# Reordering the input projection of a two-layer attention and RWKV-7 backbone

## The reference

```python
IN_SIZES = (ATTN_WIDTH, ATTN_WIDTH, ATTN_WIDTH,          # attention's q, k, v: 512 each
            RWKV_WIDTH, RWKV_WIDTH, RWKV_WIDTH,          # r, k, v of the RWKV heads: 512 each
            2 * DECAY_LORA, 2 * AAA_LORA, GATE_LORA)     # wd 64, ad 64, gd 96
r = _shift_mix(r, mu[0, 0], mu[0, 1])                    # k and v alike: a token mixes with both neighbours
v = v + (v_first - v) * jax.nn.sigmoid(v0 + (v @ v1) @ v2)      # second layer alone
kk = _heads(k * k_k)
kk = kk * lax.rsqrt(jnp.maximum(jnp.sum(kk * kk, axis=-1, keepdims=True), 1e-24))
for d in range(2):                                       # two directions
    wl = w0[d] + jnp.tanh(wd[..., d * 32:(d + 1) * 32]) @ w2[d]
    decay = jnp.exp(-jnp.exp(-jax.nn.softplus(-wl) - 0.5))
    a = jax.nn.sigmoid(a0[d] + ad[..., d * 32:(d + 1) * 32] @ a2[d])
    kd = kf * (1.0 + (a - 1.0) * k_a)
```

## Time and profile before

| | before |
|---|---|
| median of 3 runs | 2672.52 us (2670.89 to 2677.59) |
| the profiled execution | 2676.98 us, its span 2675.2 us |
| busy: PE, DVE, ACT, POOL | 91%, 62%, 45%, 6% |
| mean granted TensorE clock | 0.957 |
| DMA | 497.56 MB, 186 GB/s; 281 to 372 GB/s in the slices of the experts |
| MATMUL L635 (projection's channels) | x736, 301.6 us, 569 ns each |

### The profile page before, as it was taken

How to read it: one execution, slowest core, us unless ns; L and a number is a source line. 1 busy time by engine, 2 the same in 40 slices (tenths; PEclk the granted TensorE clock), 3 DMA queues, 4 the chain that set the end, 5 groups by cost and what they waited for, 6 DMA issues and landing times.

```text
span 2675.2 us, 47479 instructions
## 1 busy us (share of the span) xinstructions
PE 2443.7 (91%) x19717; PEld 1854.3 (69%) x19717; DVE 1664.6 (62%) x1848; ACT 1206.2 (45%) x1279; POOL 171.4 (6%) x260
## 2 busy tenths in 40 slices
PE   4998879999899999988679987999999999999998
PEld 2334459963688786445478956888888888788886
DVE  3265656543433323266645437989898888989897
ACT  2243432221222223244422215767677677767675
POOL 0000024400000000000054100000000000000000
PEclk8989899999899999989899988999999999999999
DMA  7211520033232224321000146989898989989897
GB/s 265 63 47 63 192 92 4 20 159 103 71 95 95 95 79 174 116 63 63 1 3 19 44 180 252 371 309 372 327 371 313 368 310 348 345 329 360 321 355 281
DMA packets 233284, 497.56 MB, mean 186 GB/s; under 512 B 9398, under 2 KB 78284, under 8 KB 226092
## 3 DMA queue, kind: packets, MB, share of 16 engines
q1 hardware_dynamic: 230960, 481.10, 49.8%
q10 hardware_dynamic: 2172, 14.20, 1.4%
HBM read 488.98 MB, written 6.29 MB: 185 GB/s over the span
## 4 chain that ended last, share of the span: by engine, by line
PE 81%; DVE 9%; ACT 4%; issue 3%; POOL 1%; DMA 1%; ACTq 0%; SPq 0%; DVEq 0%; POOLq 0%
PE ps L559 16%; PE ps L560 16%; PE ps L561 16%; PE ps L786 10%; PE ps L635 8%; PE ps L552 7%; PE ps L587 2%; PE ps L814 1%; ACT weight_parts L1421 1%; POOL tail L2048 1%; PE ps L610 1%; DVE tail L1601 1%; PE ps L1062 1%; PE ps L945 1%; DVE tail L1821 1%
## 5 line engine op out<-in xcount | busy, mean ns | idle before, releaser
L1956 DVE TENSOR_TENSOR weight_parts<-front,weight_parts 128x2048 fp32r<-128x2048 f32 x336 | 767.8, 2289 | 86.8 <-ACT weight_parts L1421 86.2
L1421 ACT ACTIVATE weight_parts<-front 128x2048 fp32r<-128x2048 f32 x336 | 642.2, 1918 | 246.5 <-PE ps L561 246.4
L559 PE MATMUL ps<-weight_parts,token_parts 128*128 128x512 f32 x1344 | 533.9, 397 | 16.9 <-DVE token_parts L1963 16.9
L561 PE MATMUL ps<-weight_parts,token_parts 128*128 128x512 f32 x1344 | 527.1, 392 | 0.0
L560 PE MATMUL ps<-weight_parts,token_parts 128*128 128x512 f32 x1344 | 527.1, 392 | 0.0
L635 PE MATMUL ps<-front,tail 128*128 128x512 f32 (+4 forms) x736 | 301.6, 569 | 15.9 <-DMA tail<-in_w_in 10.8
L559 PEld LDWEIGHTS ps<-weight_parts,token_parts 128*128 128x128 f32 x1344 | 254.5, 189 | 72.9 <-DVE token_parts L1963 18.8
L561 PEld LDWEIGHTS ps<-weight_parts,token_parts 128*128 128x128 f32 x1344 | 254.2, 189 | 54.8
L560 PEld LDWEIGHTS ps<-weight_parts,token_parts 128*128 128x128 f32 x1344 | 254.3, 189 | 51.1
L1143 ACT ACTIVATE tail<-ps 128x512 f32<-128x512 f32 (+2 forms) x223 | 125.8, 568 | 361.2 <-DVE tail L1739 170.5
L786 PE MATMUL ps<-tail 64*64 64x64 f32 x7808 | 257.9, 220 | 33.6 <-POOL tail L2048 15.4
(11 more groups left out here) (215 smaller groups left out, 2429.6 us busy)
## 6 DMA issues: line engine op xcount, KB each, us to landing
front<-in_exp_w SPq DMA_DIRECT2D x342, 1024.0 KB, 6.3
tail<-in_ffn_w SPq DMA_DIRECT2D x30, 1024.0 KB, 5.1
tail<-in_ada_w SPq DMA_DIRECT2D x27, 1024.0 KB, 10.1
tail<-in_w_in SPq DMA_DIRECT2D x24, 1024.0 KB, 5.1
front<-in_ada_w SPq DMA_DIRECT2D x21, 1024.0 KB, 9.8
tail<-in_w_out SPq DMA_DIRECT2D x8, 1024.0 KB, 5.1
parked_x<-front ACTq DMA_DIRECT2D x2, 2048.0 KB, 10.2
front<-parked_x ACTq DMA_DIRECT2D x2, 2048.0 KB, 9.4
```

Of the source, the lines that this page charges most:

```text
L559: mm(view, a_hi, b_hi, start=start, stop=False)
L561: return mm(view, a_hi, b_lo, start=False, stop=stop)
L1421: f_(whi[k % PARTS], at(A_RING2 + (k % RING2) * SLOT2, SLOT2), ACT.Copy).then_inc(cnt["act"].sem, 1)
L1956: ins = v.tensor_tensor(wlo[m % PARTS], at(A_RING2 + (m % RING2) * SLOT2, SLOT2), whi[m % PARTS], ALU.subtract)
```

## The change: what it does

1. SP loads the first three ring places (`lora`, `k0`, `r0`) before it waits for the modulation or the feed-forward. In the second layer the first four modulation tiles (`ada_load(4, 0..3)`) are issued behind them, where before they stood behind the last feed-forward load.
2. `wd` and `ad` become one output `wa` of 128 columns; the weights w2 and a2 share one array `lw`, so that the four products of a tile lie on four different groups of 32 rows, in banks 0 to 3, which are kept for them.
3. Order of the projection: k0, k1, r0, r1 with the first half's key norms, rates and the other keys and receptances between, then the four v, then aq and ak with the last rates, ropes and bonuses. The values `vt` move into the first four steps of attention's loop (two tiles a step), and the first layer's modulation tiles move from steps 0..15 to 3..18.
4. Key norms: `key_sums` puts the sum of each head and token on one of 16 columns (tokens on partitions), maximum, root and reciprocal run on 128x16, and `key_spread` writes them back to 64 rows each by products with the identity.
5. `rates` has its own buffers for both directions (`sigs`), all four tiles keep their own keys and receptances, the exponentials come in two steps (`growths`, `decays`) and one of five is left out (line 1274), as are two copies (1624, 1632). In the first layer bonus and value are multiplied at once, so `values` is left to the second layer.
6. In the second layer `vf` is read back after the last bonus, `lv2` is loaded late.

```diff
-        for hh in range(2):
-            proj += [(f"r{hh}", 1536 + 256 * hh, 256), (f"k{hh}", 2048 + 256 * hh, 256),
-                     (f"v{hh}", 2560 + 256 * hh, 256)]
...
+        for c0, nm in ((0, "k"), (0, "r"), (256, "k"), (256, "r"), (0, "v"), (256, "v")):
+            proj.append((f"{nm}{c0 // 256}", {"r": 1536, "k": 2048, "v": 2560}[nm] + c0, 256))
...
+                def key_sums(hh):
+
+                    bank = banks.take(pe, ("kn", l, hh))
+                    for q in range(2):
+                        pe.wait_ge(ev("kk_sq"), 4 * l + 2 * hh + q + 1)
+                        for t in range(4):
+                            at_ = 8 * q + 2 * t
+                            ins = mm(bank[:, at_:at_ + 2], ksq[:, 2 * hh + q, t * P:(t + 1) * P], onesbd[:, 0:P:CH],
+                                     start=(q == 0 and t == 0), stop=True, skip_group_check=True)
+                    banks.fill(ins, ("kn", l, hh))
+
+                def key_spread(hh):
+
+                    pe.wait_ge(ev("kn_inv"), 2 * l + hh + 1)
+                    for q in range(2):
+                        bank = banks.take(pe, ("ks", l, 2 * hh + q))
+                        for t in range(4):
+                            for h in range(2):
+                                at_ = 8 * q + 2 * t + h
+                                ins = mm(bank[CH * h:CH * h + CH, t * P:(t + 1) * P],
+                                         kinv[:, at_:at_ + 1].broadcast_to([P, CH]), ident, start=(t == 0), stop=True,
+                                         skip_group_check=True)
+                        banks.fill(ins, ("ks", l, 2 * hh + q))
...
+                    for d in range(2):
+                        for k, nm in enumerate(("wl", "al")):
+                            r = slice(64 * k + 32 * d, 64 * k + 32 * d + 32)
+                            product((nm, l, cc, d), [(lambda b: b[:, :], [(lw[r, cs_], thad[r, :])])], 2 * d + k)
...
+                banks.kept |= {0, 1, 2, 3}
+                by_channel("lora", ("wa", l), 0, P, 0)
+                if l == 1:
+                    ada_tile(4, 4)
+                by_channel("lora", ("gd", l), P, 96, t0)
+                if l == 1:
+                    ada_tile(4, 5)
+                for q in range(2):
+                    channels("k", q)
+                    if l == 1:
+                        ada_tile(4, 6 + q)
+                channels("r", 0)
+                if l == 1:
+                    ada_turn(4)
+                key_sums(0)
+                channels("r", 1)
+                key_spread(0)
+                rates(0)
+                for q in range(2):
+                    channels("k", 2 + q)
+                rates(1)
+                for q in range(2):
+                    channels("r", 2 + q)
+                key_sums(1)
+                channels("v", 0)
+                rates(2)
+                for q in range(1, 3):
+                    channels("v", q)
+                key_spread(1)
+                channels("v", 3)
...
                 for n in range(len(units) + 3):
                     if n < len(units):
                         scores(n)
+                    if n < 4:
+                        for t in range(2):
+                            values(n // 2, n % 2 * 2 + t)
...
-                    if l == 0 and n < 2 * DC:
-                        ada_tile(1 + n // DC, n % DC)
-                    if (l, n) == (0, 10):
+                    if l == 0 and n >= 3:
+                        ada_tile(1 + (n - 3) // DC, (n - 3) % DC)
+                    if (l, n) == (0, 13):
                         ada_turn(1)
...
+                for q in range(2):
+                    mix("k", q)
+                for q in range(2):
+                    keys(q)
+                if l == 1:
+                    ada_row(4)
+                for q in range(2):
+                    mix("r", q)
+                key_root(0)
+                rates(0)
+                decays(0, 0)
+                mix("k", 2)
+                decays(0, 1)
...
+                load_until(("r0", l))
                 if l == 0:
                     banks.see(sp, ("ada", 0))
                 else:
 
+                    for k in range(4):
+                        ada_load(4, k)
                     banks.see(sp, ("f2", DC - 1))
```

More of the change, by code:

```diff
@@ L592, in ada_tile @@
                     banks.fill(ins, ("ada", u))
-                    banks.kept = set()
+                    banks.kept -= {banks.where["ada", u][0]}
             def ada_turn(u):
@@ L701, in project @@
+                for q in range(2):
+                    channels("ak", q)
+                    rope("aq", 2 + q)
+                bonus(2)
+                for q in range(2):
+                    channels("ak", 2 + q)
+                    rope("ak", q)
+                bonus(3)
+                banks.kept -= {0, 1, 2, 3}
+                for q in range(2):
+                    rope("ak", 2 + q)
                 if l > 0:
@@ new lines, in attn @@
+                def attn(nm, a):
+                    dst, c0 = (qT, t0) if nm == "aq" else (kT, 0)
+                    copy_out((nm, l, a), dst[:, a, c0:NTOK], lambda b: b[:, c0:NTOK])
+                bank = banks.see(act, ("wa", l))
+                f_(thad[0:64, :], bank[0:64, :], ACT.Tanh)
+                banks.done(f_(thad[64:P, :], bank[64:P, :], ACT.Copy), ("wa", l))
+                copy_out(("gd", l), sgd[0:96, t0:NTOK], lambda b: b[0:96, t0:NTOK], func=ACT.Sigmoid)
+                for q in range(2):
+                    mix("k", q)
@@ new lines, in project @@
+                for q in range(2):
+                    keys(q)
+                if l == 1:
+                    ada_row(4)
+                for q in range(2):
+                    mix("r", q)
[4 more added lines that the diff above has]
+                decays(0, 1)
+                mix("k", 3)
+                keys(2)
+                mix("r", 2)
+                rates(1)
+                keys(3)
+                decays(1, 0)
@@ L1292, in project @@
+                mix("r", 3)
+                decays(1, 1)
+                key_root(1)
+                mix("v", 0)
+                rates(2)
+                mix("v", 1)
+                mix("v", 2)
+                decays(2, 0)
+                mix("v", 3)
+                decays(2, 1)
                 if l == 0:
@@ new lines, in project @@
+                if l == 1:
+                    modulation(4)
+                mix("r", 1)
+                key_inverse(0)
+                keys(0)
+                keys(1)
+                rates(0, 0)
+                mix("k", 2)
+                rates(0, 1)
+                bonus_in(0)
+                mix("k", 3)
+                mix("r", 2)
+                rates(1, 0)
+                mix("r", 3)
+                rates(1, 1)
+                key_floor(1)
+                bonus_in(1)
+                mix("v", 0)
@@ new lines, in project @@
+                key_inverse(1)
+                mix("v", 1)
+                mix("v", 2)
+                keys(2)
+                keys(3)
+                rates(2, 0)
+                mix("v", 3)
+                rates(2, 1)
+                bonus_in(2)
+                bonus(0)
+                bonus(1)
+                rates(3, 0)
+                rope("aq", 0)
+                rope("aq", 1)
+                rates(3, 1)
+                bonus_in(3)
+                rope("aq", 2)
+                rope("aq", 3)
```

410 lines of the change are left out of this document (181 added, 229 removed).

## The result

| | before | after |
|---|---|---|
| median | 2672.12 us (2670.89 to 2677.59, 4 runs) | 2582.64 us (2579.53 to 2587.34, 4 runs) |
| profiled execution, its span | 2676.98, 2675.2 us | 2582.96, 2581.1 us |
| mean granted clock | 0.957 | 0.971 |

The ratio is 0.9666, 95% interval 0.9651 to 0.9681: 89.5 us less. The prediction said 2587 within 2563 to 2622. The page's first part after: PE's busy time fell by 40 us (2443.7 before), and DVE's share of the chain that ended last fell from 9% to 5%.

A forecast was written before the change was run, and what follows sets the result against it. The projection was taken as bound by PE's own work, its waits for the ACT-DVE chain of the rates and the half clock behind them. Gains 48.3 + 46.4 - 10 = 84.7 us gave a median of 2587, range 2563 to 2622.

The forecast's parts named there:

- Start: First layer's projection start: early loads and joined wd and ad end `gd` at 65.2 instead of 82.6, gain 17.4 us.
- Waits: Projections: PE's waits for bonus inputs and norm squares go, 16.9 and 21.2 us; new waits cost 2.7 and 8.2.
- Key norms: Both projections: sums and spreads on PE replace the `kn` products, net cost 6.1 us a layer, between 1.1 and 10.9.
- Rates: Both projections: four row groups take 1.06 us a tile instead of 1.99, gain 3.6 us a layer, or nothing.
- Attention, first layer: First layer: `vt`'s 28 us leave the projection, attention grows by 17.4 and about 1.9 us; net gain 8.7 us.
- Attention, second layer: Second layer: `vt`'s 28 us leave the projection, attention grows from 45.2 to 58 us; net gain 15, between 10 and 18.
- Clock: Projections: one new half-clock stretch a layer, behind short waits and key norms, at 4.9 us: 10 us charged.
- Rival A: Each of the four key norms brings a half-clock stretch losing 6.5 us: 26 us instead of 10, so 2603; chance 0.17.
- B: Projections: fixed ACT and DVE order makes a piece late in each half, 30.7 us of waits return: about 2630; chance 0.13.
- C: Bank starvation: PE waits for DVE at each of 16 rates passes; at 6.5 us each, 2691, slower; chance 0.04.
- D: The clock gates stay open: no new half clock and cheap key norms, 2565; chance 0.06.
- E: No gain: attention's loops lengthen by all of `vt` and waits move, within 0.3% of before; chance 0.02.

The follow-up runs named there:

- e5: The kernel before the change, with only the first layer's first three ring loads issued ahead of the modulation wait; 2663.20 against 2674.33 us.
- e1: The changed kernel with the ring loads back behind the waits in both layers and the second layer's first four modulation tiles at their old place; 2593.63 us.
- e9: The changed kernel with the product of v3 made twice in each layer, 13.8 us more work on PE; 2602.88 us.
- e8: The changed kernel with root and reciprocal before r1's mix, banks 0 to 3 kept, k3 mixed before the bonus input, step 11's modulation row read earlier; 2569.04 us.
- e3: The changed kernel with each layer's eight value tiles in one block ahead of attention's loop; 2598.29 us.
- e4: The changed kernel with the difference of the running sum made three times, 22.2 us more work on DVE; 2596.26 us.
- e6: The changed kernel with the first half's key root on ACT and its reciprocal on DVE ahead of the mix of r1; 2576.28 us.
- e2: The changed kernel with the key norms on 128x512 again (ones product, root, reciprocal), at the new places; 2614.82 us.
- e10: The kernel of e8, with the rates' named banks no longer setting the bank turn back; 2566.09 us.
- e7: The changed kernel with banks 0 to 3 kept behind the modulation, so the second layer's r0 doesn't take bank 1; 2583.34 us.

## Why the prediction was right, step by step

- **Start.** Said: `wa` ends near 58, `gd` near 65, 17.4 us. Measured: `gd` 65.6, 17.0 us. e5 and e1 show the loads' share: 11.4 us in the old form, 6.8 in the new. With the loads there in time ACT's norm sets the start, as 2.52 us of waiting show in after (for L1256) and in e5 (for L1217, the same operation in before); in e1 PE waits 10.75 us for the load again.
- **Waits.** The 38.1 us of rows 1 and 2 are gone. New ones, said and measured: first layer's root 2.7 and 2.6; in the second layer r0 behind the modulation 3.2 and 3.4, the root 2.3 and 2.4, r3 on the bank of k3 1.6 and 1.4, small ones 1.1 and no new one. In the projections every one stands where the walk along banks and queues had it.
- **Key norms: right in kind, too dear.** Sixteen sums take 1.84 us, 1.71 by the pace to the next row, 0.11 us each instead of 0.15; thirty-two spreads 1.97, by pace 0.06 each instead of 0.075. A layer's norms are 2 x (1.71 + 1.89) = 7.2 us, net 3.7 where I charged 6.1. The nearest row, a transpose of 128 columns, was an upper bound for two columns, and I read it too high: 0.60 us is the row's length with the end of its last instruction, and the next row starts at 335.04, 0.53 us after 334.51, so by pace it is 0.13 each. The rule that I weighed (the Trainium skill, "TensorEngine Tiling (Array Packing)", Instruction Overhead) would have made the 32 sums under 1 us; they are 3.4, so here the trace disagrees with it.
- **Rates.** 1.14 us a tile instead of 1.99, 1.07 by pace: said 1.06. The first tile of a layer stands at half clock in after (2.09 us in the first layer, 3.03 in the second); the second layer's still takes 2.08 at full clock in e9, and what holds it there stays open.
- **Attention, first layer.** The first four steps took 258.08 - 226.69 = 31.4 us (said 32.7). The whole took 95.5 where 73.4 + 19.3 = 92.7 was said. The step that was missing is the wait of 3.66 us at 286.51: `ada_tile(2, 0)` takes the bank of the modulation just finished, and ACT reads that row only at the end of step 11, behind its exponentials. I had counted `ada_row(2)` and `ada_turn(2)` at the loop's end and not asked which bank the next row takes in the middle. With ACT's reading moved ahead, in e8, the same wait is 0.22 us.
- **Attention, second layer: mis-sized.** It went from 47.5 to 64.8 us, 17.3 more where 13 was said, so the gain was 10.7 instead of 15, near the lower end that I gave (10). The term that was wrong is its half clock: I took what before lost there as gone (25 for the rest instead of 29.0), but PE is busy for 12.8 us at half clock in after's, which costs 6.4, and before lost 6.3. The windows of after:

```profile
1183.70:1187.60 3.90, 3.90 (x10) 2.04 (x10) 1.55 (x3) 2.13 (x3) 0.00 (x0) 0.50 0.00 0
1228.60:1232.00 3.40, 3.40 (x12) 1.92 (x10) 1.30 (x3) 2.54 (x7) 0.00 (x0) 0.50 0.00 0
1235.40:1242.20 6.80, 5.46 (x16) 4.23 (x16) 1.85 (x5) 2.46 (x7) 0.00 (x0) 0.50 0.00 0
```

- **Clock: the sum near, the split by luck.** I charged 4.9 us a layer. In the first projection one stretch of 3.4 us cost 1.7; in the second the stretches at 1051, 1065 and 1181 cost 1.7, 3.4 and 1.5 (as far as the scores), 6.6 together. The one at 1065 is missing behind the same wait in e3, e4 and e9. Rival A, a loss behind each of the four norms, is refuted: the second norms (154.65 in the first layer) have no wait before them and run at full clock, and in e6 all four do. The reading of the Trainium skill that I had put beside that rival ("TensorE: Matmul & The Clock Gate", The HAM clock gate) doesn't carry it there.
- **Sum.** With these sizes the first layer is 17.0 + 16.9 + 10.5 - 3.7 + 3.4 - 2.6 - 1.7 + 5.9 = 45.7 us (46.7 measured), the second 7.1 + 21.2 + 13.8 - 3.7 + 3.4 - 7.2 - 6.6 + 10.7 = 38.7 (39.7 measured). That the sum came within 2 us of the 86.4 is partly luck, since the errors of the terms largely cancelled: the norms (4.8 us in all) and the first layer's clock (3.2) were too dear, attention too cheap (2.8 and 4.3) and the second layer's clock too (1.7). The median lies 4.4 us below the forecast: its gain is 89.5 us, 1.7 of the difference to 84.7 lies in the edited stretches and the rest in the unedited ones, which no step of mine foresaw.
- **The other rivals.** B (a piece late in each half) and C (each pass of rates late) have no row in after. But e2 and e4 show how close they were: with the reciprocals left wide, 33 us of waits of B's kind stand in e2's two projections. The sentence "DVE and ACT finish each piece before PE needs it" holds for the whole change, but for the waits named above, and not for the reordering with wide norms. D (2565: no new half clock, cheap norms) is where e8 and e10 arrive, once the new waits are gone as well; E (no gain) has nothing for it.

## What to carry to other kernels

When an order is changed so that one engine never waits, the other engines' queues lose their slack: work that was cheap in the old order (here 128x512 reciprocals, 17 us) becomes dear in the new (32 us), so a reordering and a lightening of the side engines have to be costed together. Walk the new order with the buffer that every product takes, to the end of every loop that was shifted: all new waits over 1 us in the projections were found that way, and the largest missed one (3.66 us) was in a loop where the walk had stopped early. A wait that is removed upstream is worth something only if the next taker's buffer is free earlier too (e7). A wait of 2.4 us can cost more than twice that when half clock follows it, but whether it follows differs between kernels with the same wait (e6, e9), so one trace doesn't price it.

## What the hardware showed beside this

- **A matmul with two moving columns isn't free.** 128x128 f32 weights with two moving columns pace at 0.11 us an instruction at full clock, half of the 0.223 us of 256 columns.
- **Four row groups beat two.** The same eight 32-row f32 instructions of 512 columns took 1.99 us on two row groups and 1.14 us on four.
- **Code that is not touched moves too.** The unedited stretches have two lengths each, 2.8 and 4.9 us apart, in kernels with the same instructions there. For the second it goes with how the half clock falls in the experts' first products: in before it is one stretch of 37.6 us (from 1592.4), and so in all ten traces with the greater length; in after two of 10.2 and 23.9 us with 3.4 us at full clock between them (from 1501.7), and so in e7 and e10, the other two with the lesser. What decides that stays open. Each kernel has one trace, and the executions of one kernel differ as much (before 2670.9 to 2677.6 us, after 2579.5 to 2587.3), so the length may belong to the execution and not to the kernel. It sets a floor of some 8 us under a comparison of two traces here, and it is a part of why e3's, e4's and e9's medians lie above what their edited stretches did.
